# Attention stages of a two-layer decoder trunk: heads in pairs, mask and maximum in one instruction, other orders and buffers

## What is computed

```python
def banded_attention(q, k, v, max_dist, sinks=None):
    ...
    s = jnp.einsum('bhgnqd,bhnkd->bhgnqk', qb, kband) * (hd ** -0.5)
    s = jnp.where(mask, s, NEG)
    m = jnp.max(s, axis=-1, keepdims=True)
    m = jnp.maximum(m, sk)                     # layer 1
    e = jnp.exp(s - m)
    den = jnp.sum(e, axis=-1, keepdims=True) + jnp.exp(sk - m)
    p = e / den
    o = jnp.einsum('bhgnqk,bhnkd->bhgnqd', p, vband)
```

## Time and profile before

| | us |
|---|---|
| median of 3 runs (1452.98 to 1455.34) | 1455.18 |
| the profiled execution | 1454.9 |
| its span | 1453.1 |
| TensorE busy in the span | 1384.4 |
| VectorE, ScalarE, GpSimdE busy | 795.8, 349.6, 307.8 |
| mean granted clock of TensorE | 0.978 |

### The profile page before, as it was taken

One profiled execution on the slowest core, in us unless ns is written; L12 is line 12 of the kernel. 1 busy time (PEld: TensorE's weight loads), 2 busy tenths in 40 slices (PEclk: granted clock), 3 DMA queues, 4 the chain that ended last, 5 costly groups with the idle time before them and its releaser, 6 DMA issues.

```text
span 1453.1 us, 17104 instructions
## 1 busy us (share of the span) xinstructions
PE 1384.4 (95%) x6288; PEld 1124.2 (77%) x6288; DVE 795.8 (55%) x1077; ACT 349.6 (24%) x733; POOL 307.8 (21%) x358
## 2 busy tenths in 40 slices
PE   6999998999999999999999886999999999999997
PEld 5887785688677888888888775878677888888886
DVE  5897866336556453244436768727565443344434
ACT  4338133412332110001112133623331110001113
POOL 1221213212311212211211113322311221221220
PEclk9999998999999999999999987999999999999998
DMA  5332331032322332233233220013223233233221
GB/s 188 99 88 86 88 102 44 15 102 90 114 73 89 100 101 93 96 102 94 94 102 94 94 88 15 1 59 99 76 73 100 89 101 101 88 101 101 90 99 73
DMA packets 90241, 127.16 MB, mean 88 GB/s; under 512 B 5440, under 2 KB 53824, under 8 KB 90176
## 3 DMA queue, kind: packets, MB, share of 16 engines
q1 hardware_dynamic: 90176, 126.27, 27.5%
HBM read 124.15 MB, written 2.10 MB: 87 GB/s over the span
## 4 chain that ended last, share of the span: by engine, by line
PE 75%; DVE 14%; issue 6%; DMA 3%; POOL 2%; ACT 0%; SPq 0%; DVEq 0%; POOLq 0%; ACTq 0%
PE ps L489 22%; PE ps L493 22%; PE ps L492 22%; PE ps L624 3%; DVE w_lo L854 2%; PE ps L591 2%; PE ps L607 1%; DVE xc L1087 1%; POOL prob L442 1%; POOL w_hi L450 1%; DVE acc L875 1%; DVE h L894 1%; DVE rope L928 1%; DVE xc L1145 1%; DVE rope L926 1%
## 5 line engine op out<-in xcount | busy, mean ns | idle before, releaser
L854 DVE TENSOR_TENSOR w_lo<-raw,w_hi 128x1024 fp32r<-128x1024 f32 x226 | 280.2, 1241 | 482.0 <-POOL w_hi L450 479.9
L450 POOL TENSOR_SCALAR w_hi<-raw 128x1024 fp32r<-128x1024 f32 x226 | 249.1, 1102 | 990.8 <-DMA raw<-in_w_gate_up 414.0
L489 PE MATMUL ps<-z_hi,w_hi 128*128 128x512 f32 x1040 | 409.8, 394 | 17.8 <-DVE w_lo L854 9.0
L492 PE MATMUL ps<-z_lo,w_hi 128*128 128x512 f32 x1040 | 406.2, 391 | 0.0
L493 PE MATMUL ps<-z_hi,w_lo 128*128 128x512 f32 x1040 | 406.1, 391 | 0.0
L489 PEld LDWEIGHTS ps<-z_hi,w_hi 128*128 128x128 f32 x1040 | 196.3, 189 | 62.6 <-issue 8.0
L489 PE MATMUL ps<-f_hi,w_hi 128*128 128x512 f32 x608 | 238.3, 392 | 1.0 <-issue 0.7
L493 PE MATMUL ps<-f_hi,w_lo 128*128 128x512 f32 x608 | 236.6, 389 | 0.0
L492 PE MATMUL ps<-f_lo,w_hi 128*128 128x512 f32 x608 | 236.6, 389 | 0.0
L492 PEld LDWEIGHTS ps<-z_lo,w_hi 128*128 128x128 f32 x1040 | 196.3, 189 | 42.0 <-issue 1.4
L493 PEld LDWEIGHTS ps<-z_hi,w_lo 128*128 128x128 f32 x1040 | 196.2, 189 | 40.9
(11 more groups left out here) (180 smaller groups left out, 1195.6 us busy)
## 6 DMA issues: line engine op xcount, KB each, us to landing
raw<-in_w_gate_up SPq DMA_DIRECT2D x176, 256.0 KB
raw<-in_w_down SPq DMA_DIRECT2D x44, 512.0 KB
raw<-in_w_in SPq DMA_DIRECT2D x28, 512.0 KB
raw<-in_w_out SPq DMA_DIRECT2D x20, 512.0 KB
raw<-in_xa_wkv SPq DMA_DIRECT2D x16, 512.0 KB
raw<-in_xa_wq SPq DMA_DIRECT2D x8, 512.0 KB
raw<-in_xa_wo SPq DMA_DIRECT2D x8, 512.0 KB
raw<-in_w_qkv SPq DMA_DIRECT2D x8, 512.0 KB
```

Of the source, the lines that this page charges most:

```text
L450: pool.tensor_scalar(w_hi[:, slot], raw[:, slot], 1.0, 1.0, ALU.mult, ALU.mult).then_inc(s_hi, 1)
L489: ins = pe.matmul(o, whi, rhi, start=start, stop=False)
L492: pe.matmul(o, whi, rlo, start=False, stop=False)
L854: dve.tensor_tensor(w_lo[:, slot], raw[:, slot], w_hi[:, slot].bitcast(F32), ALU.subtract).then_inc(s_lo, 1)
```

## The change

Head pairs: in the two mixers the values of heads n and n+1 are multiplied together, their matmuls interleaved one by one; in layer 1 the scores too (layer 0 has one set of score banks). The values of a pair come in odd iterations. In all attention stages transposes now come ahead of the values in an iteration. The fused instruction `tensor_tensor_reduce` makes (scores + mask) x (-scale) and its running minimum, one per block of 128 queries, so four per head; the masks are scaled on the host. Score banks are free when all four are done (`s_read` is `s_max`). In layer 0 VectorE now copies 768 of the 1280 transposed columns. `prob_t` has three buffers, four in layer 1. Layer 1's order is query product 0, keys and values, memory transposes, query product 1; rotations of tiles 4 to 7 are in iterations 2, 4, 6 and 8; the key units are one each in iterations 0 to 3, in layer 0 too, and are copied out in iteration 3.

```diff
-        STAGES += [("qkv_q0", 1, 4), ("qkv_q1", 1, 4), ("mem_t1", 1, 0), ("qkv_kv", 1, 2), ("attn1", 2, 2), ("out1", 2, 4)]
+        STAGES += [("qkv_q0", 1, 4), ("qkv_kv", 1, 2), ("mem_t1", 1, 0), ("qkv_q1", 1, 4), ("attn1", 2, 2), ("out1", 2, 4)]
...
-            a["t_dve"] = a["t_width"] if plan == "attn0" else (a["t_width"] - 1) // BANK * BANK
-            a["copies"] = 1 if plan == "attn0" else 2
+            a["t_dve"] = BANK
+            a["fill_n"], a["told_turn"] = (3, 2) if a["pairs"] else (1, 0)
...
+            z_turned, a["t_bufs"] = z_zh + 12 * a["width"], 4 if plan == "attn1" else 3
...
+                a["s_" + s] = a["s_max"] if s == "read" and a["masks"] else sem(f"s_{name}_{s}")
...
                 for n in range(ATTN[name]["heads"]):
                     normalise(ATTN[name], n)
-                    if n == 0:
-                        high(first + 4, first + 6)
-                    if n == 1:
-                        high(first + 6, first + 7)
+                    if n <= 2:
+                        high(first + 4 + n, first + 5 + n)
...
+                def scores(*heads):
...
+                    if heads[-1] >= a["s_bufs"]:
+                        pe.wait_ge(a["s_read"], heads[-1] - a["s_bufs"] + 1)
                     for i, k0_, nk, c in a["scores"]:
+                        for n in heads:
+                            b0 = BANK * (a["bank"](0) + 2 * (n % a["s_bufs"]))
+                            ins = pe.matmul(flat[:, b0 + c:b0 + c + nk], q(n)[:, i * P:(i + 1) * P],
+                                            key(n)[:, k0_:k0_ + nk], start=True, stop=True)
...
+                def values(*heads):
+                    pe.wait_ge(a["s_pt"], 2 * (heads[-1] + 1))
...
                     for x_, (j, src, q0_, nq, start) in enumerate(a["values"]):
+                        for n in heads:
+                            r0 = rows * (n % a["per"])
+                            ins = pe.matmul(ps[r0:r0 + rows, a["o_banks"][tile % 2], q0_:q0_ + nq], value(n, j),
...
-                for n in range(H + 3):
-                    if n < H:
+                for n in range(H + 4):
+                    if n < H and not (a["pairs"] and a["s_bufs"] == 2):
                         scores(n)
+                    elif n < H and n % 2 == 0:
+                        scores(n, n + 1)
                     if n in extra:
                         pe.wait_ge(s_free[(g + 1) % 2], free_needed(g + 1))
                         extra[n]()
-                    if n >= 3:
-                        values(n - 3)
+                    if a["pairs"] and n >= 5 and n % 2:
+                        values(n - 5, n - 4)
                     if 2 <= n < H + 2:
                         turns(n - 2)
+                    if not a["pairs"] and 3 <= n < H + 3:
+                        values(n - 3)
...
-                      {0: lambda: memory_keys(0, (0, 1)), 1: lambda: memory_keys(0, (2, 3))}, ahead(*out0), (8, 9))
+                      {j: lambda j=j: memory_keys(0, (j,)) for j in range(4)}, ahead(*out0), (10, 11))
...
-                        for c, w, mc in a["masks"]:
-                            ins = dve.scalar_tensor_tensor(prob[n % 3][:, c:c + w], flat[:, b0 + c:b0 + c + w], a["scale"],
-                                                           mask[:, mc:mc + w], ALU.mult, ALU.add)
-                        ins.then_inc(a["s_read"], 1)
...
+                        first = neg_sinks[:, n:n + 1] if a["sink"] else -NEG
+                        for i, (c, w, mc, pc) in enumerate(a["masks"]):
+                            ins = dve.tensor_tensor_reduce(a["prob"][n % 3][:, pc:pc + w], flat[:, b0 + c:b0 + c + w],
+                                                           mask[:, mc:mc + w], -a["scale"], first, ALU.add, ALU.min,
+                                                           st[:, 1, i:i + 1])
+                        ins.then_inc(a["s_max"], 1)
+                        return
...
+                    if n == a["fill_n"]:
+                        for b in range(2):
+                            dve.wait_ge(a["s_filler"], b + 1)
+                            dve.tensor_copy(dst[:, BANK * b:BANK * (b + 1)],
+                                            ps[:, a["o_banks"][b], :]).then_inc(a["s_filled"], 1)
+                    low_to(u0 + {0: 4, 2: 6, 3: 7, 5: 8}.get(n, 0))
...
-                    attention(ATTN["attn1"], {1: lambda: [rotate_q(6), rotate_q(7)]})
+                    low_to(q1_unit + 7)
+                    for t in range(4, 8):
+                        qkv1(q1[:, t, :], s_done["qkv_q1"], "qkv_q1", t - 4)
+
+                    attention(ATTN["attn1"], {2 * t - 6: lambda t=t: rotate_q(t) for t in range(4, 8)})
```

More of the change, by code:

```diff
@@ L114, in attention_plan @@
         blocks = [(0, 0)] + [(i, j) for i in range(1, TB) for j in (i - 1, i)]
-        return dict(width=TB * 2 * P, scores=scores, reduces=[(P, 1, P), (2 * P, TB - 1, 2 * P)],
-                    masks=[(P, (2 * TB - 1) * P, P)], probs=[(start[i], P if i == 0 else 2 * P) for i in range(TB)],
+        return dict(width=TB * 2 * P, scores=scores, masks=[(start[i], P if i == 0 else 2 * P, start[i], start[i]) for i in range(TB)], probs=[(start[i], P if i == 0 else 2 * P) for i in range(TB)],
                     turns=[(2 * P * i + P * (j - i + 1), P * n) for n, (i, j) in enumerate(blocks)],
@@ L307, in trunk @@
                 a["output_at"][n + (4 if n + 4 < heads else 3)] = tile
[L308 removed]
+            a["prob"] = [at(f"prob_{name}{i}", [P, a["width"]], F32, z_zh + 4 * a["width"] * i) for i in range(3)]
+            z_turned, a["t_bufs"] = z_zh + 12 * a["width"], 4 if plan == "attn1" else 3
+            a["prob_t"] = [at(f"prob_t_{name}{i}", [P, a["t_width"]], F32, z_turned + 4 * a["t_width"] * i)
+                           for i in range(a["t_bufs"])]
+            assert z_turned + 4 * a["t_width"] * a["t_bufs"] <= z_raw
+            for s in ("scores", "max", "read", "exp", "rden", "prob", "turned", "pt", "head", "o_hi", "o_lo",
                       "filler", "filled"):
[L310 removed]
+                a["s_" + s] = a["s_max"] if s == "read" and a["masks"] else sem(f"s_{name}_{s}")
             ATTN[name] = a
@@ L606, in turns @@
                     for src, dst in a["turns"]:
-                        ins = pe.transpose(flat[:, t0 + dst:t0 + dst + P], prob[n % 3][:, src:src + P], ident[:])
-                        if n == 0 and (src, dst) == a["turns"][0]:
+                        ins = pe.transpose(flat[:, t0 + dst:t0 + dst + P], a["prob"][n % 3][:, src:src + P], ident[:])
+                        if n == a["told_turn"] and (src, dst) == a["turns"][0]:
                             ins.then_inc(s_used, 1)
                     ins.then_inc(a["s_turned"], 1)
-                def values(n):
-                    pe.wait_ge(a["s_pt"], a["copies"] * (n + 1))
-                    tile = n // a["per"]
-                    if n == 0:
+                def values(*heads):
+                    pe.wait_ge(a["s_pt"], 2 * (heads[-1] + 1))
+                    tile = heads[0] // a["per"]
+                    if heads[0] == 0:
@@ L616, in values @@
                         pe.wait_ge(a["s_filled"], 2)
-                    if n % a["per"] == 0 and tile >= 2:
+                    if tile >= 2:
                         pe.wait_ge(a["s_o_lo"], tile - 1)
                     rows = P // a["per"]
-                    r0 = rows * (n % a["per"])
-                    o = ps[r0:r0 + rows, a["o_banks"][tile % 2], :]
                     last = len(a["values"]) - 1
                     for x_, (j, src, q0_, nq, start) in enumerate(a["values"]):
-                        ins = pe.matmul(o[:, q0_:q0_ + nq], value(n, j), prob_t[n % 2][:, src:src + nq],
-                                        start=start, stop=x_ == last)
@@ L626, in values @@
-                    ins.then_inc(a["s_head"], 1)
-                for n in range(H + 3):
-                    if n < H:
+                        for n in heads:
+                            r0 = rows * (n % a["per"])
+                            ins = pe.matmul(ps[r0:r0 + rows, a["o_banks"][tile % 2], q0_:q0_ + nq], value(n, j),
+                                            a["prob_t"][n % a["t_bufs"]][:, src:src + nq], start=start, stop=x_ == last)
+                            if x_ == last:
+                                ins.then_inc(a["s_head"], 1)
```

177 lines of the change are left out of this document (71 added, 106 removed).

## The result

The changed kernel takes 1434.73 us (median of 4 runs, 1432.61 to 1439.05) against 1455.11 us, a ratio of 0.9867, 95% interval 0.9847 to 0.9888. It is faster by some 20 us; the forecast was 1422, 33 us faster. The time lies in the forecast's range and the direction is right, but the gain was forecast more than one and a half times too large. The profiled execution after is 1432.61 us long (span 1430.7), so the two traces differ by 22.4 us.

A forecast was written before the change was run, and what follows sets the result against it. TensorE, busy 95% of the span, was taken as the bound; gains of 25 us in layer 1, 8 in layer 0 and 1 in cross-attention sum to 34 off 1454.9, forecast 1422 us, range 1406 to 1446.

The forecast's parts named there:

- B: Rival: paired score halves overlap but value halves don't, 12 us more, 1434 us; chance 0.14.
- C: Rival: neither scores nor values of a pair overlap; scores add another 14 us, 1448 us; chance 0.06.
- m: VectorE's fused mask-and-maximum pass per head: taken as 1.7 us in layer 1 and 2.1 in layer 0.
- +0.1 each: Extra time per fused instruction for its accumulated result, from ScalarE's accumulator read of 188 ns, half of it hidden.
- D: Rival: fused pass runs at half rate, 25 x 0.9 = 22 us more, 1444 us; chance 0.08.
- E: Rival: each fused instruction costs a fixed 0.9 us, 47 us more, 1469 us, slower than before; chance 0.06.
- on chains: Range ends: 25 fused passes set the pace, so shorter passes give 11 us less, longer ones 12 more.
- 5.1 + m = 6.8: Layer 1 pair without rotation: scores, fused pass, denominator, normalisation, transposes and hand-overs take 6.8 us against 8.6 before.
- 5.5 + 2m = 8.9: Layer 1 pair with a rotation: VectorE is the chain, 8.9 us; TensorE waits 3.7 us, three times.
- plus 4: Layer 0 attention: 4 us added for slow clock to 69.6 us, giving 73.6 and a gain of 8.
- I add 7: Layer 1: 7 us added for half clock behind gaps, twice 3.4 us, giving 131 us and a gain of 25.
- The walk: Layer 0's eight heads stepped through with VectorE's low parts: waits 2.4, 3.0, 1.4 (heads 3, 5, 7), 2.2 in smaller ones.

The follow-up runs named there:

- the kept-busy run: The changed kernel with ScalarE's output ahead, plus TensorE multiplying the identity before six heads' transposes in layer 1 instead of idling: 1425.92 us, ratio 0.9810 (base 1424.72).

## Why the prediction was right and where it was wrong

**Do two heads overlap? Right.** Both halves do, at the price of one head. As lengths of pieces: a pair's scores 1.79 against one head's 1.78, its values 1.75 against 1.74, and in layer 0 2.37 against 2.37. Rivals B and C fall. The Trainium skill (TensorEngine Tiling (Array Packing), Theoretical Speedup) promises up to 2x for columns of at most 64; the trace agrees, with 1.75 us for a pair's values against 1.74 for one head's in the earlier trace rows. B's price for value halves that don't overlap (12 us) is near what taking the overlap away costs (9.6). C's added 14 for scores apart is wrong: it costs 0.9.

**The fused pass. Right in kind, m too large.** It takes 1.57 us per head in layer 1 and 1.74 in layer 0, where 1.7 and 2.1 stood. Over the low ends of 1.2 and 1.68 that is 0.09 and 0.015 for each of the four instructions: the "+0.1 each" fits layer 1 and not layer 0. The two differ in the start value of the minimum: with 256 columns an instruction takes 0.48 us where it is read from a tensor (neg_sinks, layer 1) and 0.42 where it is a constant. In layer 1 the instructions of 256 columns start every 0.405 us. Rivals D and E fall with it. The Trainium skill (Vector Engine (DVE) Microarchitecture Reference, Points that are easy to get wrong) has a half rate for a scalar-tensor-tensor form with two non-bf16 sources in SBUF. The fused pass has one in PSUM: 256 columns every 0.405 us are 1.6 ns a column with the start of each instruction in it, against 1.2 for the plain pass of the earlier trace rows, which is not half rate; no run here has both sources of it in SBUF. The forecast gave the pass no line of its own in the sum; taken away it costs 18.0 us, more than any other part that was taken away. The 25 passes "on chains" behind the ends of the range are too many: 13.3 us in layer 1 at 0.88 us a pass and 5.6 in layer 0 at 1.66 are some 18 (an estimate from the stretches of that run).

**Order q, kv, q. Right.** The waits of 3.77 and 4.44 us are gone, and one of 2.79 stands ahead of the value transposes, forecast at 2.3.

**"5.1 + m = 6.8" for a pair without rotation. This step failed.** It left out the tile's output. ScalarE had it ahead of the exponentials before and has it behind them now, and VectorE, in program order, takes f_lo before the next fused pass: the pair shown above takes 8.51 us. With ScalarE's output moved it takes 6.47; the forecast's own sum at the measured m = 1.57 gives 6.7. The other pair without a rotation takes 8.01 us for another reason, the slower clock: its scores last 3.36 us, f_lo is done 0.1 us before they end, and moving the output changes nothing in it.

```profile
898.34 3.36 PE L592 MATMUL ps<-k,q 64*128 64x128 f32 x16 [1.13 <-DVE stat L977]
```

**"5.5 + 2m = 8.9" with a rotation. The chain and the waits right, the period too short.** Measured 10.95, 11.10 and 10.23. VectorE is the chain, as forecast: the scores behind each of the three wait for the fused pass (1.13, 0.36 and 1.13 us). TensorE's waits in the three are 11.4 us in all, where 3 x 3.7 = 11.1 stood; its work is 20.9 us where 15.7 stood, since 10.0 us of it ran at the slower clock and lost 5.0 (0.82 granted over the three), the scores taking 3.36 us in two of the three. In the middle one, whose scores took 1.79, VectorE took f_lo and a low part of 1.22 us ahead of the fused pass, which the sum doesn't have; of the low parts that VectorE waits for among the first heads (9.5 us between 845 and 915) it had 2 us in all. In the last version (clock up, low parts later, ScalarE copying), these pairs take 8.6, 8.9 and 8.2.

**The clock. Under-sized.** In layer 0 "plus 4": 13.7 us, all busy, ran at 1.2 GHz, which is 6.8 us of lost work. In layer 1 "I add 7": 20.0 busy us in five pieces, 10 us lost. As a sum, layer 1 has 26.4 us of waits where 24.1 stood and 10 of lost clock where 7 stood, which makes up the 5 us missing there. These rows of the changed kernel are the three pieces of layer 0:

```profile
222.45:225.86 3.41, 3.41 (x17) 3.41 (x17) 2.62 (x4) 0.00 (x0) 0.75 (x1) 0.50 0.40 138
242.93:246.34 3.41, 3.41 (x9) 1.00 (x10) 1.82 (x9) 0.21 (x2) 0.85 (x3) 0.50 0.00 0
256.58:263.41 6.83, 6.83 (x20) 2.28 (x18) 1.82 (x9) 1.08 (x4) 3.04 (x6) 0.50 0.00 0
```

For layer 0 this is nearly the whole miss: its waits were put at 9.0 us and are 9.4, its gain is 4.8 and not 8, and 2.8 of the 3.2 missing are the clock's. Lost clock is not simply added to the time: part of it lies in waits, as the kept-busy run shows in layer 1 and the two cross-attentions below show again.

**Layer 0's waits. Right in sum, by luck.** The walk had 2.4 us ahead of head 3, 3.0 ahead of head 5 and 1.4 ahead of head 7, with a pass of 2.1 us. The waits are 0.5, 2.2 and 3.3 there, and 3.4 elsewhere, with a pass of 1.74: the places and the pass are wrong and the sum agrees. The walk had VectorE's low parts in it, but not that they can be moved. One is here, in the changed kernel: VectorE idle for 3.20 us at a low part of an output unit that TensorE starts only at 272.09, 49 us later.

```profile
223.24 1.23 DVE L861 TENSOR_TENSOR w_lo<-raw,w_hi 128x1024 fp32r<-128x1024 f32 x1 [3.20 <-POOL w_hi L451]
```

**Cross-attention, "1 us". Wrong in sign.** Transposes ahead of the values cost 0.6 us each; the order turned back gives that back. The lower bound of -1.5 held it.

**The sum.** 34 became 22.4 in the traces: 5 of the miss in layer 1, 3 in layer 0, 2 in the cross-attentions, 1 elsewhere. (34 off the 1455.2 of the runs is 1421, not 1422.) What the forecast had in kind holds; it mis-sized the slower clock behind TensorE's waits, by some 6 us in the two layers, and left out what stands in VectorE's queue beside the chain. Some luck is in it: m was 0.13 and 0.36 us too large, which for 11 passes in layer 1 and 8 in layer 0 hides up to 4 us (an estimate) of what was put too small. The shared copies of layer 0 and the added buffers, forecast at zero, were not taken out in any run.

## What to carry to other kernels

The parts of such a change don't add up. Alone on the kernel before, where TensorE paces, the fused pass gives 5.5 us and the order 6.0; taken out of the changed kernel, where in layer 1 a chain over VectorE paces, they cost 18.0 and 15.4 (the latter with the key units spread), while the paired scores, which save 13 us of TensorE's time, are worth 0.9. So once a change has moved the bound, write out the new pacing engine's queue in program order, with every instruction that is not of the chain in it: the two largest gains left here (10 and 12 us) were such bystanders, an output that waited for another engine's exponentials and low parts that nobody needed yet. And a wait of TensorE is to be counted with the slower clock behind it.

## What was unexpected of the hardware

GpSimdE's normalisation of one head takes 1.73 us, and 2.68 where VectorE runs a rotation at the same time. The first row is beside fused passes, the second beside a rotation:

```profile
877.25 1.73 POOL L443 TENSOR_SCALAR prob_attn<-prob_attn,stat 128x128 f32<-128x128 f32 x4 [2.40 <-DVE stat L992]
...
893.49 2.68 POOL L443 TENSOR_SCALAR prob_attn<-prob_attn,stat 128x128 f32<-128x128 f32 x4 [3.41 <-DVE stat L992]
```

It is not the rotation alone. In the version with the low parts later the same normalisation takes 2.74 us, 1.0 more than 1.73, beside a low part of 1.22 us:

```profile
883.28 2.74 POOL L443 TENSOR_SCALAR prob_attn<-prob_attn,stat 128x128 f32<-128x128 f32 x4 [3.23 <-DVE stat L992]
...
883.55 1.22 DVE L861 TENSOR_TENSOR w_lo<-raw,w_hi 128x1024 fp32r<-128x1024 f32 x1
```

The low part and three of the four instructions of a rotation read two tensors from SBUF; the fused pass reads one and PSUM. No run here takes them one by one.

TensorE's clock did not follow the length of the last wait alone. In both cross-attentions of the changed kernel TensorE first waits 0.93 and then 2.81 us, at the same places; in the first the granted clock stayed at 1.00 (the row of its stretch above), in the second, whose row follows, it was 0.96. What decides that stays open. Both stretches last 40.0 us all the same: behind the slower pieces the next wait is 0.45 us, where it is 1.81 in the first.

```profile
996.38:1036.37 39.99, 35.80 (x154) 26.93 (x153) 19.83 (x29) 11.90 (x39) 12.53 (x21) 0.96 0.20 66
```
